# Splitting the fourth round's weights ahead of the first round's evacuation, and sine and cosine in the third quarter

## The reference

```
mod  = silu(c) @ w_ada + b_ada                      # six rows of 1024: sh1, sc1, g1, sh2, sc2, g2
h    = rms_norm(x, norm1_gain) * (1 + sc1) + sh1
proj = h @ w_in                                     # split into hq, hf, hi, hg, aq, ak, av, gate_h, gate_a
y_h  = hgrn2_branch(hq, hf, hi, hg) @ w_hg_branch   # a gated recurrence in chunks of 64 tokens
y_a  = swa_branch(aq, ak, av) @ w_attn_branch       # attention in a window; q and k are normed per head and rotated
x    = x + g1 * ((sigmoid(gate_h) * y_h + sigmoid(gate_a) * y_a) @ w_out)
x    = x + g2 * moe_ffn(h2)                         # 32 experts, top 4
```

## Time and profile before

| | |
|---|---|
| median of 3 runs | 1552.63 us (1552.29 to 1553.14) |
| the profiled execution's own time | 1555.04 us |
| its span in the profile | 1553.2 us, mean granted TensorE clock 0.987 |
| PE busy | 1456.3 us, 94% of the span |
| PEld busy | 766.0 us, 49% |
| DVE busy | 605.9 us, 39% |
| ACT busy | 346.7 us, 22% |
| HBM read | 592.66 MB, 382 GB/s over the span |

### The profile page before, as it was taken

The page is one execution under the profiler, slowest core; times in us unless marked ns, Lnnn a source line. Parts: engine busy times, 40 slices in busy tenths (PEclk is TensorE's granted clock), DMA queues, the critical chain, the costliest instruction groups (busy, mean ns, idle before and its releaser), DMA issues.

```text
span 1553.2 us, 21045 instructions
## 1 busy us (share of the span) xinstructions
PE 1456.3 (94%) x8762; PEld 766.0 (49%) x8762; DVE 605.9 (39%) x940; ACT 346.7 (22%) x407; POOL 8.7 (1%) x20
## 2 busy tenths in 40 slices
PE   8999999999899999999998999999989999998677
PEld 6768985333233333333332333333338999854343
DVE  4786684232123232232231321322337687522111
ACT  4763332010011010110110110101023383421110
POOL 0000100000000000000000000000000000000000
PEclk9999999999998999999999999999999999999889
DMA  9895589999999999999999999999996445999998
GB/s 381 357 409 202 194 335 395 428 429 428 429 427 411 429 429 427 429 428 429 426 430 428 429 425 430 427 429 427 428 427 241 181 163 222 374 412 427 427 427 339
DMA packets 46587, 594.74 MB, mean 383 GB/s; under 512 B 5388, under 2 KB 5516, under 8 KB 10552
## 3 DMA queue, kind: packets, MB, share of 16 engines
q1 hardware_dynamic: 44624, 588.76, 90.7%
q0 software_dynamic: 1312, 4.34, 0.8%
q10 hardware_dynamic: 584, 0.64, 0.1%
HBM read 592.66 MB, written 1.06 MB: 382 GB/s over the span
## 4 chain that ended last, share of the span: by engine, by line
PE 56%; DMA 37%; DVE 4%; issue 1%; ACT 1%; SPq 0%; DVEq 0%; ACTq 0%
PE PS L614 51%; DMA ring<-in_w_up 29%; DMA arena<-in_w_gate_e 3%; DMA arena<-in_last_down 3%; DMA arena<-in_w_up_e 2%; PE PS L794 2%; DVE ring_r L395 1%; PE PS L814 1%; PE PS L1523 1%; DVE arena L904 1%; PE PS L730 1%; PE PS L1533 0%; DVE arena_r L395 0%; DMA consts<-in_first 0%; SPq L1127 0%
## 5 line engine op out<-in xcount | busy, mean ns | idle before, releaser
L614 PE MATMUL PS<-ring,arena 128*64 128x512 f32 x3020 | 671.5, 597 | 39.7 <-DMA ring<-in_w_up 31.8
L614 PEld LDWEIGHTS PS<-ring,arena 128*64 128x64 f32 x3020 | 210.5, 137 | 463.0 <-issue 393.8
L614 PE MATMUL PS<-arena 128*128 128x128 f32 (+12 forms) x1240 | 229.7, 443 | 2.9 <-DVE arena L2168 0.9
L892 DVE TENSOR_SCALAR arena<-PS 128x512 f32<-128x512 f32 x32 | 22.1, 691 | 480.6 <-PE PS L614 480.6
L593 ACT ACTIVATE arena<-arena 128x512 f32<-128x512 f32 x32 | 20.2, 630 | 697.6 <-DVE arena L892 697.6
L614 PE MATMUL PS<-ring_r 128*128 128x256 f32 (+1 forms) x576 | 170.6, 306 | 0.2
L614 PEld LDWEIGHTS PS<-arena 64*128 64x128 f32 (+6 forms) x1240 | 109.0, 166 | 121.1 <-issue 115.6
L614 PE MATMUL PS<-hT_r,ring_r 128*128 128x256 f32 x832 | 156.9, 287 | 3.3 <-DVE ring_r L395 3.3
L614 PEld LDWEIGHTS PS<-hT_r,ring_r 128*128 128x128 f32 x832 | 132.8, 194 | 8.9 <-issue 7.5
L395 DVE TENSOR_TENSOR ring_r<-ring,ring_r 128x2048 fp32r<-128x2048 f32 (+1 forms) x54 | 119.0, 2212 | 30.7 <-ACT ring_r L390 29.6
L390 ACT ACTIVATE ring_r<-ring 128x2048 fp32r<-128x2048 f32 (+1 forms) x54 | 99.5, 1846 | 103.0 <-PE PS L614 101.0
(11 more groups left out here) (372 smaller groups left out, 996.1 us busy)
## 6 DMA issues: line engine op xcount, KB each, us to landing
ring<-in_w_up SPq DMA_DIRECT2D x128, 2048.0 KB, 21.9
ring<-in_w_down SPq DMA_DIRECT2D x59, 2048.0 KB, 19.8
ring<-in_w_in SPq DMA_DIRECT2D x17, 2048.0 KB, 10.1
ring<-in_w_gate_e SPq DMA_DIRECT2D x11, 2048.0 KB, 35.6
ring<-in_w_down_e SPq DMA_DIRECT2D x10, 2048.0 KB, 27.0
ring<-in_w_up_e SPq DMA_DIRECT2D x10, 2048.0 KB, 29.8
ring<-in_w_ada SPq DMA_DIRECT2D x6, 2048.0 KB, 13.9
arena<-in_w_gate_e SPq DMA_DIRECT2D x5, 2048.0 KB, 23.8
```

The source lines that it names most:

```text
L614: return nc.tensor.matmul(o, w, m, start=first, stop=last)
L892: V.tensor_scalar(glu.rearrange("p (kk b q) -> p kk b q", kk=4, b=2), hu[:, :, :, :, 0], 7.0, None, ALU.min)\
```

## The change

`split_upper(12)` is issued by ScalarE right behind the opening, before the copy of round 0's result and before the squares. On VectorE `split_lower(12)` stands before `head_norm`, and `split_lower(13)` takes its place as the `meanwhile` of `head_norm`, so that it comes before the reciprocal and no longer behind the gains. Sine and cosine are computed in the third quarter of the opening (q == 2), behind `split_upper(8)`, and not behind the fourth. No instruction is added or taken out on these engines by the source, and no transfer and no TensorE instruction is touched.

```diff
@@ -1231,9 +1231,11 @@
                 upper_part(q)
                 split_upper(act, OPENING * q + 1)
                 split_upper(act, OPENING * q + 2)
-            act.wait_ge(S("angles"), 2)
-            A(sm("sin"), sm("rr"), ACT.Sin).then_inc(S("sincos"), 1)
-            A(sm("cos"), sm("rn"), ACT.Sin).then_inc(S("sincos"), 1)
+                if q == 2:
+                    act.wait_ge(S("angles"), 2)
+                    A(sm("sin"), sm("rr"), ACT.Sin).then_inc(S("sincos"), 1)
+                    A(sm("cos"), sm("rn"), ACT.Sin).then_inc(S("sincos"), 1)
+            split_upper(act, 12)
             aux = [0]
 
             def aux_bank():
@@ -1252,7 +1254,6 @@
             act.wait_ge(S("big_free_A"), 1)
             act.wait_ge(S("big_free_V"), 1)
             A(at(A1MAP, "qkT"), at(A1MAP, "qk"), ACT.Square).then_inc(S("qk_squares"), 1)
-            split_upper(act, 12)
 
             act.wait_ge(S("att_ms"), 1)
             nc.scalar.sqrt(sm("rsa", 24), sm("ssa", 24)).then_inc(S("att_std"), 1)
@@ -2104,9 +2105,9 @@
                         last = TV(qk[:, i, a:a + n, :], qk[:, i, a:a + n, :], bc_mid(sm(g_), n), ALU.mult)
                 return last
 
-            L(head_norm(qk, 12, at(A1MAP, "qkT"), [(0, 8, "q_gain"), (8, 4, "k_gain")], 1, lambda: split_lower(v, 12),
+            split_lower(v, 12)
+            L(head_norm(qk, 12, at(A1MAP, "qkT"), [(0, 8, "q_gain"), (8, 4, "k_gain")], 1, lambda: split_lower(v, 13),
                         True))
-            split_lower(v, 13)
 
             v.wait_ge(S("sincos"), 2)
             rt_ = at(A1MAP, "rt")
```

## The result

The changed kernel takes 1558.76 us in the median of 7 runs (1556.78 to 1561.29) where the kernel before takes 1553.14 us (7 runs, 1552.26 to 1557.54). The ratio is 1.0033, with a 95% interval from 1.0019 to 1.0046. I had forecast 1552.8 us, no change, within 1549.6 to 1555.0.

A forecast was written before the change was run, and what follows sets the result against it. Bound: the experts' transfers, whose start waits for PE's dense part of block 1. 2.7 + 0.2 us gained at round 3, 3.1 us lost at the scores: 1552.63 + 0.2 = 1552.8 us, range 1549.6 to 1555.0.

The forecast's parts named there:

- the bound and where it is read: Experts' transfers fill the DMA engines; a microsecond PE gains or loses in the first 250 us reaches the end whole.
- sine and cosine at no cost: Third quarter of the opening: table load and two activations, 1.63 us, fit in ACT's 1.93 us idle; no gain.
- round 3 without a wait: After `ada(4)`: PE starts round 3 at 61.2, not 63.96 us, so 2.7 us gained.
- PE's lead: From round 3 to the scores: PE 2.7 + 0.2 = 2.9 us ahead.
- the order of the next releases: Behind the second pair of scores: VectorE's and PE's steps alternate as before; `split_lower(18)` lets round 6 begin at 113.8.
- a wait of 3.1 us that was not there: Ahead of the second pair of scores: PE waits 3.1 us for line 2163, and the whole 2.9 us are gone.
- all 0.2 us later: From the second pair of scores on: steps continue as before, 0.2 us later at round 6 and at the end.
- The clock's fall in it: Rival, chance 0.20: clock drops in the new gap before the second pair of scores; +1.6 us (1554.2) or +3.3 us (1555.9).
- the dearer price, 1555.9: Clock rival's longer drop, laid over round 5: 3.4 us lost, +3.3 us in sum; chance 0.07.
- VectorE's lateness: Behind `split_lower(13)` in `head_norm`: idle 2.1 us for 1.71, line 0.4 us later; bounds of extra idle 0.2 to 0.6.
- The drain: Table load ahead of the square root: about 1.38 us more would make VectorE 0.6 us late; left out of the sum.
- B: Rival theory of the experiments, no chance given: slowness comes from clock drops in experts and block 2, differing between runs.

The follow-up runs named there:

- the pieces alone: The change without its sine and cosine edit (only pieces 12 and 13 moved), against the kernel before: ratio 1.0016 (1.0002 to 1.0030).
- the third profile of the change: Third measurement of the unedited changed kernel, against the kernel before: ratio 1.0013 (1.0002 to 1.0023).
- the filled gap: The changed kernel plus 15 small identity products on PE between `ada(8)` and the second pair of scores, against the kernel before: ratio 0.9995.
- the second profile of before: The unedited kernel before, run again as its own pair against the kernel before: ratio 0.9995 (0.9980 to 1.0009).
- 13 behind the gains: Piece 12 ahead as in the change, `split_lower(13)` left behind the gains, against the kernel before: ratios 0.9984 and 0.9991 in two measurements.
- the kernel with VectorE delayed: The kernel before plus three memsets on VectorE ahead of the first evacuation of scores, against the kernel before: ratio 1.0075 (1.0058 to 1.0091).

## Why the prediction was wrong

**Right**: the bound and where it is read, so far as the profiles reach (2.3 us late at the experts' start, 3.1 us at the end of the span); sine and cosine at no cost (0.29 us to spare, 0.3 foreseen); `split_upper(12)` at the release of piece 9's buffer; round 3 without a wait; nothing gained by it at the scores, because PE's lead ends in a wait for line 2163; the order of the next releases.

**The step that failed** is the sum's last one, "a wait of 3.1 us that was not there", followed by "all 0.2 us later". I took a wait of PE as costing its length and nothing more. The clock's fall in it I had as a rival with a chance of 0.20. It was there in all three profiles of the change and in that of the pieces alone, and it goes when the gap is filled. Without the drop the sum was nearly right, +0.62 us at round 6 for +0.2; with it, round 6 came 2.6 to 4.1 us late. It should have been the forecast.

**The rival itself was priced in the wrong place.** I laid the drop over round 5, where PE has 0.3 us of slack, and got +1.6 us or +3.3 us. It lay first of all over the second and third pairs of scores, which VectorE awaits: 1.13 us became 2.08 us, twice, 1.75 us in VectorE's line with no slack to eat. Even the dearer price, 1555.9, lies 2.9 us below the measured 1558.76. Over round 5 it came on top: in the third profile of the change, with 0.50 up to 104 us, round 6 was 4.1 us late, while VectorE's line was 2.5 us late.

**Two terms that were mis-sized.** The new wait was 3.82 us, not 3.1. One part of the difference is PE's lead: at `ada(8)` it was 3.28 us (32.68 us behind the start of `ada(4)`, before 35.96), not 2.9. From start to start the waits of before had cost more than their idle time: 2.80 us for the one of 2.73, and 0.48 us for the one of 0.26 inside round 3. The other part is VectorE's lateness, 0.4 us by the sum, 0.72 us measured; its extra idle, 2.46 less 1.71 us, is 0.75 us and outside the bounds of 0.2 to 0.6 us. The idle ahead of `split_lower(13)` was 2.46 us, not 2.1, because `split_upper(13)` started 0.41 us behind the square root and not 0.13 as before. Of it 0.19 us stand as "issue" in the timeline. Before, the root had not waited for `att_ms` and now it had (1.17 us idle); that this is why its successor came later is my reading and was not tried. With the clock up, the lateness alone made the +0.62 us of the filled gap; the lead was lost in the wait in any case.

**A page, weighed again.** The drain that the Trainium skill, ScalarE: Activation LUTs, section What ACT_TABLE_LOAD costs, adds to a table load is not seen here either: the load at 42.84 took 1.28 us, to 44.12, and the sine followed at 44.14.

**What stays open** is the size. The change comes 2.3 to 4.2 us late to the experts' start (195.1, 195.1 and 197.0 against 192.8), yet the three measurements say 5.6, 1.0 and 1.8 us in the medians. The 192.8 is itself one execution with a drop at 137 to 146 us. From round 6 to the experts' start that profile took 138.5 us. Of the other profiles with this drop four took 138.1 to 138.2 us and one 136.8; without it seven took 136.5 to 137.2 and one, with a deeper drop at 235 to 250 us, 139.8. So the drop of 137 to 146 us seems to cost some 1 to 2 us at the experts' start, and against the second profile of before, which lacks it (192.3), the change is 2.8 to 4.7 us late. Such drops come and go: at 137 to 146 us in 6 of the 14 profiles, at 235 to 250 us in 12 of them, and more in block 2. The kernel before also pays for its old gap in some executions. From the experts' start to the end of the span the three profiles of the change took 1301.8, 1299.4 and 1301.6 us, for the same instructions. So B is true of the spread and not of the lateness at the scores; how much of the time of a whole run belongs to the drop behind the gap is not shown. Why the first measurement came out higher than the two others was not settled; the runs of the kernel before reach from 1551.05 to 1560.87 us over the chips used.

## What to carry to other kernels

Taking a wait away from TensorE pays only as far as the next release that is not its own: follow the other engine's line to that point first, and if the change makes that line later, the gain is not merely lost. Where the lead must pile up as idle time, ask what the clock will do there and what stands behind it: here it was short products that another engine waited for, and their slowness went into that engine's line in full. Move the work so that both lines come earlier (here: one piece ahead, the other left in its place), or fill the gap with products that nobody reads. With the runs taken here both show in the profiles (1.3 us ahead at round 6, and the clock at 1.00); in the time of the whole kernel they are at the edge of what could be measured.

## What the runs showed of the hardware

Whether the clock falls behind the same gap differs between executions: around 2.7 us of standstill it fell in three of four profiles, around 3.8 us in four of four, and behind 1.7 us and 0.9 us with one pair of scores between in the one that had them. The 0.94 us between the later pairs alone, as in before, left it at 1.00 in each, and so did the 1.67 us inside round 3, with dense products on both sides, in both profiles of 13 behind the gains. It also falls where the profile shows no idle PE, at 137 to 146 us, during or just behind the small products of the recurrence (0.62 in the mean of that window in the first profile of before), and such a drop comes and goes between executions of the same instructions; of the two profiles of before, one has that drop and not the one at 62 to 68 us, the other the reverse. The Trainium skill, TensorE: Matmul & The Clock Gate, Part 1, puts the lower level down to missing activity and says of the rise to the upper one that its moment varies from run to run. The drops at the gaps agree with the first, and the rises, 44.6, 45.9 and 47.8 us behind `ada(4)` in the three profiles of the change, with the second; why the clock fell at 137 to 146 us, with PE busy 9.00 of 9 us, no run here shows.

In the kernel with VectorE delayed, each memset that waited for its predecessor's semaphore cost VectorE 0.39 us of idle time on top of its 1.34 us.
